# Expert weights in halves for the last two units, and two weight loads moved ahead of the token gathers

## The reference

```python
t = h2.reshape(T, D)                       # 512 x 1024
# group of 4, then top 2 of its 8 experts -> combine (T, 32), two entries per row
for e in range(N_EXPERTS):                 # 32
    hid = jax.nn.silu(t @ w_gate_exp[e]) * (t @ w_up_exp[e])     # 1024 -> 256
    y = y + combine[:, e:e + 1] * (hid @ w_down_exp[e])          # 256 -> 1024
```

## Time and profile before

| | us |
|---|---|
| median of 3 runs | 719.07 |
| lowest and highest | 716.56 and 719.19 |
| the profiled execution | 716.74 |
| its span on the core | 714.8 |
| TensorE busy in it | 651.9 (91%) |
| mean DMA rate over the span | 240 GB/s |

### The profile page before, as it was taken

The page is one execution under the profiler, slowest core; times in us unless marked ns, Lnnn a source line. Parts: engine busy times, 40 slices in busy tenths (PEclk is TensorE's granted clock), DMA queues, the critical chain, the costliest instruction groups (busy, mean ns, idle before and its releaser), DMA issues.

```text
span 714.8 us, 7294 instructions
## 1 busy us (share of the span) xinstructions
PE 651.9 (91%) x2526; PEld 313.5 (44%) x2526; DVE 381.5 (53%) x751; ACT 179.5 (25%) x366; POOL 90.2 (13%) x112
## 2 busy tenths in 40 slices
PE   0599999999999999999979999889999899898993
PEld 0454644444344444455644555434344443333331
DVE  3955265998877674417872338842323252232258
ACT  1430111133233434441121222112221121121132
POOL 1012312210011111000000000113111112111012
PEclk9999999999999999999999999999999999998997
DMA  9990826060602415070194028699999999999962
GB/s 324 393 378 6 273 81 235 0 235 0 206 31 83 153 25 212 1 244 29 37 387 195 29 77 335 247 417 419 415 423 419 420 418 418 420 419 420 412 262 117
DMA packets 50405, 171.85 MB, mean 240 GB/s; under 512 B 10176, under 2 KB 10176, under 8 KB 37440
## 3 DMA queue, kind: packets, MB, share of 16 engines
q1 hardware_dynamic: 42544, 159.24, 57.2%
q0 software_dynamic: 6016, 10.53, 3.9%
q10 hardware_dynamic: 1808, 1.61, 0.7%
HBM read 168.20 MB, written 13.64 MB: 254 GB/s over the span
## 4 chain that ended last, share of the span: by engine, by line
PE 75%; DMA 7%; DVE 7%; issue 6%; POOL 2%; ACT 1%; SPq 1%; DVEq 0%; ACTq 0%; POOLq 0%
PE psum L669 29%; PE psum L939 13%; PE psum L965 8%; PE psum L816 7%; DMA ring<-in_w_down_exp 4%; DVE work L1288 2%; PE psum L773 2%; PE psum L919 2%; DMA work<-h_rows,tok_t 2%; PE psum L793 2%; PE psum L781 1%; PE psum L738 1%; PE psum L731 1%; DMA posi<-in_positions 1%; PE psum L747 1%
## 5 line engine op out<-in xcount | busy, mean ns | idle before, releaser
L669 PE MATMUL psum<-ring,hT 128*128 128x512 f32 (+1 forms) x576 | 234.6, 561 | 0.0
L669 PEld LDWEIGHTS psum<-ring,hT 128*128 128x128 f32 x576 | 102.7, 191 | 119.2 <-issue 118.8
L939 PE MATMUL psum<-ring,hT 128*64 128x512 f32 (+1 forms) x352 | 84.9, 594 | 1.4 <-issue 1.4
L1700 DVE TENSOR_SCALAR work<-work 128x256 f32<-128x256 f32 x18 | 5.2, 291 | 121.0 <-PE psum L949 96.1
L939 PEld LDWEIGHTS psum<-ring,hT 128*64 128x64 f32 (+1 forms) x352 | 29.2, 142 | 54.6 <-issue 54.4
L1288 DVE SCALAR_TENSOR_TENSOR rows<-ring,sm,rows 128x512 f32<-128x512 f32 x64 | 51.3, 802 | 1.7
L965 PE MATMUL psum<-ring,work 128*64 128x512 f32 (+1 forms) x176 | 45.5, 620 | 3.3 <-DMA ring<-in_w_down_exp 2.6
L1184 ACT ACTIVATE work<-psum 128x256 f32<-128x256 f32 x18 | 6.9, 385 | 155.1 <-PE psum L939 155.1
L939 PE MATMUL psum<-rows,hT 128*64 128x512 f32 (+1 forms) x80 | 39.8, 656 | 6.6 <-issue 6.6
L1812 POOL TENSOR_TENSOR both_bufs<-both_bufs 128x256 f32<-128x256 f32 (+1 forms) x28 | 18.9, 673 | 180.4 <-DVE both_bufs L1349 156.7
L1349 DVE TENSOR_TENSOR both_bufs<-psum,cosT 128x512 f32<-128x512 f32 (+1 forms) x24 | 14.7, 614 | 48.9 <-PE psum L669 38.2
(11 more groups left out here) (270 smaller groups left out, 860.6 us busy)
## 6 DMA issues: line engine op xcount, KB each, us to landing
ring<-in_w_gate_exp SPq DMA_DIRECT2D x22, 1024.0 KB, 23.0
ring<-in_w_up_exp SPq DMA_DIRECT2D x22, 1024.0 KB, 26.0
ring<-in_w_down_exp SPq DMA_DIRECT2D x22, 1024.0 KB, 27.0
ring<-in_w_in SPq DMA_DIRECT2D x8, 2048.0 KB, 9.8
ring<-in_w_ada SPq DMA_DIRECT2D x8, 2048.0 KB, 14.8
ring<-in_w_ada SPq DMA_DIRECT2D x7, 1024.0 KB, 14.2
both_bufs<-in_w_gate_exp SPq DMA_DIRECT2D x5, 1024.0 KB, 27.0
both_bufs<-in_w_up_exp SPq DMA_DIRECT2D x5, 1024.0 KB, 28.8
```

The lines of the kernel that those rows point to most:

```text
L669: mm = pe.matmul(o[:, 0:width], hT3[:, k, b * P:(b + 1) * P], w[:, k, :], start=(k == 0), stop=(k == KD - 1))
L939: mm = pe.matmul(o[rows, :], XT[u % 2][:, k, rows], both(SLOT_OF[place])[:, k, :, :], start=(k == 0), stop=(k == KD - 1))
```

## The change

Two edits, both in what SyncE issues, with one new wait on TensorE.

The gate matrix of slot 4 is issued as soon as h2_ready and mod_done allow, and the down matrix of slot 1 behind `h2_out` and `res_sq`, both before the waits for the gathers; the up and down matrices of slot 4 stay behind them.

For units 16 and 17 gate and up of both places are loaded in halves of the contraction: first k = 0 to 3 of gate and up for both places, counted on `gu_in`, then k = 4 to 7, counted on the new `gu_rest`. `gate_up` of these units waits for `gu_rest` ahead of its product with k = 4.

```diff
+HALVED = NU - 2
...
+        gu_rest = [sem(f"gu_rest{i}") for i in range(NU - HALVED)]
...
+        def load_half(sp, e, s, part, signal):
 
-            w = KD * F
+            w = KD * F // 2
             at = gate_and_up(s)
-            sp.dma_start(at[:, 0:w], pick(wg_d, e)).then_inc(signal, 16)
-            sp.dma_start(at[:, w:2 * w], pick(wu_d, e)).then_inc(signal, 16)
+            for m, weights in enumerate((wg_d, wu_d)):
+                sp.dma_start(at[:, (2 * m + part) * w:(2 * m + part + 1) * w],
+                             pick(weights, e)[:, part * w:(part + 1) * w]).then_inc(signal, 16)
...
+            sp.wait_ge(h2_ready, NB)
+            sp.wait_ge(mod_done, 8)
+            load_gate(sp, RING, RING, gu_in[RING])
             sp.wait_ge(h2_out[1], 16 * (NB // 2))
             sp.wait_ge(res_sq, NB)
+            load_down(sp, 1, 1, down_in[1])
             for u in range(GATHERS):
                 sp.wait_ge(xg_in[u], 16)
-            load_down(sp, 1, 1, down_in[1])
-            sp.wait_ge(h2_ready, NB)
-            sp.wait_ge(mod_done, 8)
-            load_gate_up(sp, RING, RING, gu_in[RING])
+            load_up(sp, RING, RING, gu_in[RING])
             load_down(sp, RING, RING, down_in[RING])
...
+                    if UNIT_OF[place] < HALVED:
+                        sp.wait_ge(gu_mm, u + 1)
+                        load_gate_up(sp, named[place], SLOT_OF[place], gu_in[SLOT_OF[place]])
+                if LET_IN.get(u, []) and UNIT_OF[LET_IN[u][0]] >= HALVED:
                     sp.wait_ge(gu_mm, u + 1)
-                    load_gate_up(sp, named[place], SLOT_OF[place], gu_in[SLOT_OF[place]])
+                    for place in LET_IN[u]:
+                        load_half(sp, named[place], SLOT_OF[place], 0, gu_in[SLOT_OF[place]])
+                    for place in LET_IN[u]:
+                        load_half(sp, named[place], SLOT_OF[place], 1, gu_rest[UNIT_OF[place] - HALVED])
...
                 for k in range(KD):
+                    if u >= HALVED and k == KD // 2:
+                        pe.wait_ge(gu_rest[u - HALVED], 32 * len(UNITS[u]))
```

More of the change, by code:

```diff
@@ L481, in build, with load_gate, load_up @@
         SUM_BANK = (2, 4, 0, 6)
+        def load_gate(sp, e, s, signal):
+            sp.dma_start(gate_and_up(s)[:, 0:KD * F], pick(wg_d, e)).then_inc(signal, 16)
+        def load_up(sp, e, s, signal):
+            sp.dma_start(gate_and_up(s)[:, KD * F:2 * KD * F], pick(wu_d, e)).then_inc(signal, 16)
         def load_gate_up(sp, e, s, signal):
-            w = KD * F
+            load_gate(sp, e, s, signal)
+            load_up(sp, e, s, signal)
+        def load_half(sp, e, s, part, signal):
+            w = KD * F // 2
             at = gate_and_up(s)
-            sp.dma_start(at[:, 0:w], pick(wg_d, e)).then_inc(signal, 16)
-            sp.dma_start(at[:, w:2 * w], pick(wu_d, e)).then_inc(signal, 16)
+            for m, weights in enumerate((wg_d, wu_d)):
+                sp.dma_start(at[:, (2 * m + part) * w:(2 * m + part + 1) * w],
+                             pick(weights, e)[:, part * w:(part + 1) * w]).then_inc(signal, 16)
         def load_down(sp, e, s, signal):
```

## The result

The changed kernel takes 713.4 us in the median of 20 runs (710.86 to 716.78), the kernel before 717.26 us beside it (714.96 to 720.8, 20 runs). The ratio is 0.9947, 95% interval 0.9931 to 0.9963: 3.8 us faster. The profiled execution of the changed kernel took 715.57 us, with a span of 713.6.

The account below looks back on a forecast made before the run. The end was taken as set by the landing of the expert weights plus TensorE's work after it. Halves 2.6 us and early start 1.7 make 4.3 off the median 719.07: 714.8 us, range 711.8 to 718.6.

Parts of the forecast that it names:

- The early loads: Two 1 MB loads issued before the gathers: 5.0 us moved, of which the weight stream gains 1.7 us.
- the gather keeps its 3 us: First gather, clear of the two moved loads by 1.4 us, was still to take about 3.1 us.
- the hole: DMA queue dry from about 460 to 462.5 us, before the loads gate_up(0) frees; takes 3.3 of the 5.0 us.
- The halves: Units 16 and 17: 16 of 32 gate_up passes run before the second halves land; 2.6 us gained from this alone.
- The new tail: TensorE's end: gate_up(17) to end at 674.65 us, where it ended at 679.47, and down(17) at 684.7 against 688.99.
- The two pauses in gate_up(17): gate_up(17) was to wait 1.5 us for its first halves and 1.7 us for its second.
- The small rows: Half loads have 4 KB rows instead of 8 KB: 0.6 us cost in all, bounds 0 and 1.7.
- the 16 us: Upper cost of eight more DMAs by the Trainium skill's rule of about 2 us fixed cost each; prediction disagreed.
- The issues of SyncE: Eight added load issues, about 0.4 us each unloaded, were to cost nothing in front of a full queue.
- The last load: Last down load, read as landing at 680.4 us, was to land at 679.3, with down(17) starting at 681.05.
- The clock: Rival, chance 0.13: TensorE's clock falls in the tail after gate_up(17)'s two pauses; gain only 1.1 to 2.6 us.
- The collision with the gathers: Rival, chance 0.07: moved loads run into the gathers, gate_up(0) starts up to 5.6 us late; end 1.4 us later.

Follow-up runs that it names:

- e6: Changed kernel, but gate_up(16) and gate_up(17) wait for both halves before their first product; ratio 1.0005 against the kernel before.
- e10: The same kernel as e6, timed and profiled once more; ratio 0.9986 against the kernel before.
- e1: Changed kernel with only the halves, the first loads back behind the gathers; ratio 0.9967 against the kernel before.
- e5: Changed kernel with all four held-back loads ahead of the waits for the gathers; ratio 1.0002 against the kernel before.

## Why the prediction was right

The result, 3.8 us, lies 0.5 us from the forecast of 4.3, inside its own range, and the profile gives 4.0. The forecast time of 714.8 us is 1.4 too high for another reason: it was counted from 719.07, the median of three runs, where the median of twenty is 717.26. Step by step:

- **The early loads, 1.7 us.** Measured alone 1.8. Every part of that sum stood in the profile: the loads end before the gather, the gather keeps its 3 us, the hole opens, speed is back about 2.5 us after the issue at 464.50. That one early load does as well as two, and a third nothing, shows that the gain is the time to the freed loads and not the megabytes moved.
- **The halves, 2.6 us.** Measured alone 2.5. The new tail, moved by the 2.8 us by which this execution's gather came late, was to have gate_up(17) end at 674.65 + 2.8 = 677.45 and down(17) at 684.7 + 2.8 = 687.5; it has 677.70 and 687.83. The two pauses in gate_up(17) were to be 1.5 and 1.7 us and are 1.45 and 1.53.
- **The small rows, 0.6 us.** 0.5 to 0.7 by the profiles of the two kernels that wait at the start, 0.65 by the rate over most of the halves. The medians allow about twice that. Neither is near the 16 us that the prediction set against it.
- **The issues of SyncE cost nothing.** They took place in front of a full queue, as forecast; unit 16's last down load went out at 661.10, 11.8 us later than before (2.8 of it the later gather), and still landed 18.0 us after, in its turn: 1.0 us sooner than before when counted from the gather, where 1.1 was forecast.
- **The last load.** Here the working read a row wrongly. It took the last down load, issued at 654.10, to land after 26.3 us, at 680.4. Two loads of that form were issued, at 653.67 and 654.10, and the trace has a time to landing for one of them only. The first row is of the kernel before, and the other two are of the kernel with the early loads alone, in which the two were issued at 654.70 and 655.12:

```profile
L492 SPq DMA_DIRECT2D ring<-in_w_down_exp x2: 333/2406/4479, 653.7 to 654.1; - x2
DMA to landing us min/median/max: 26.3/26.3/26.3
```

```profile
L508 SPq DMA_DIRECT2D ring<-in_w_down_exp x2: 333/2402/4472, 654.7 to 655.1; - x2
DMA to landing us min/median/max: 26.3/27.4/28.4
```

So 26.3 us belong to the first load, which landed at 680.0, and 28.4 to the last, which landed at 682.5; the last event of its landing stands at 682.49 in the trace. Counted from the gather's issue it then landed at 234.0 us before and at 232.8 in the changed kernel (684.09 less 451.27): 1.2 us sooner, where 1.1 was forecast. The shift was right, and the place from which it was counted was 2.1 us too early. With 682.5 - 1.1 = 681.4 in the place of 679.3, down(17) starts at 681.4 instead of 681.05 and ends at 685.05, a gain of 3.9 instead of 4.3; the profile has 4.0. In the changed kernel down(17) waited for that load and started at 684.18, where 681.4 + 2.8 is 684.2:

```profile
662.34 21.75 DMA ring<-in_w_down_exp
684.18 3.65 PE psum L991 x16
```

The reads of pair_rows, issued at 677.70 instead of 682.42 and so before the last landing, did not slow it. In e6 and e10 they go out later, 1.7 us before that landing, and the last load still takes its 21.7 us and lands at 232.8 and 232.9 from the gather. The rows of e6:

```profile
L508 SPq DMA_DIRECT2D ring<-in_w_down_exp x2: 375/1638/2900, 659.9 to 660.4; - x2
DMA to landing us min/median/max: 19.7/20.7/21.7
...
680.39 2.04 SPq L673 DMA_DIRECT2D ring<-pair_rows  x4
```
- **The rivals.** The clock did not fall in the changed kernel's tail: two pauses of 1.5 us with 3.6 us of work between them left it at 1.00 in all seven profiles that have them. The collision with the gathers was a true danger at 1.4 us of distance, as the kernel with three shows, but not for two loads.

## What to carry to other kernels

When a stream of transfers is the bound, as here, moving loads ahead pays only the time until the next load whose buffer is still in use; look for that load first, since it tells how much is worth moving and what else would have to be freed. A product whose operand lands in halves ends half a product after the landing, which is worth having only for the last consumers of the stream. To compare two profiles of kernels that share a long prefix, measure from the last event up to which both run alike. Where a row speaks for two loads, find out which one it times before a sum is built on it.

## What the runs showed of the hardware

The executions of the two kernels come in steps about 2.1 us apart: the kernel before near 715.2, 717.2 and 719.2 us, the changed one near 711.4, 713.5 and 715.7. The steps of some others, e1 and e5 above all, are less clear. The profiles show one place where such a step arises, in the short products between the output projection and the table of tokens. Windows of the kernel before and then of the changed one; the third number from the end is TensorE's granted clock:

```profile
434.00:436.00 2.00, 2.00 (x4) 0.86 (x3) 1.76 (x12) 0.22 (x1) 0.53 (x1) 0.59 1.01 426
436.00:438.00 2.00, 2.00 (x4) 0.81 (x3) 1.69 (x10) 0.00 (x0) 0.00 (x0) 0.56 1.00 352
438.00:440.00 2.00, 2.00 (x6) 0.81 (x5) 1.86 (x14) 0.21 (x1) 0.00 (x0) 1.00 0.97 383
```

```profile
434.00:436.00 2.00, 2.00 (x11) 2.00 (x11) 0.68 (x1) 0.29 (x1) 0.53 (x1) 0.50 1.01 426
436.00:438.00 2.00, 2.00 (x4) 0.97 (x4) 1.69 (x11) 0.22 (x1) 0.00 (x0) 0.50 1.00 397
438.00:440.00 2.00, 2.00 (x3) 0.73 (x3) 1.69 (x10) 0.00 (x0) 0.00 (x0) 0.50 0.89 342
```

In the second the clock stays at 1.2 GHz (0.50) until after 440 us, in the first until before 438. From SyncE's first load of this stage (425.36 and 426.11) to the gather's issue it is 23.09 us in the one and 25.16 in the other. Of the twelve profiles of this study seven have 23.1 us there, four 25.2 and one 25.5: a step of 2.1 us in between. The low clock goes with it: from 426 to 442 us it adds up to 3.4 us or to none in the seven profiles with 23.1, and to about 10 us in the other five. It is not the change: of the ten kernels with early loads five have 23.1, and the step is there when the first moved load goes out, 13.6 us after the stage's first load in the five with the longer stretch and 10.2 to 11.5 in the other five. A second shift lies before this stage: its first load was issued between 423.67 and 426.50 us in the twelve profiles, and where that arises was not looked for. The gain moves all the steps alike, and nothing that was varied here sets the step on which an execution falls, so that the medians of 12 executions of one kernel, e6 and e10, could lie 1.1 us apart. The Trainium skill, "TensorE: Matmul & The Clock Gate", says in its Part 1 that the same kernel runs a different number of its products at the low clock from run to run. It says so of a kernel's start; here the low stretch lies in the middle, and the twelve profiles agree: they have none, 3.4 or about 10 us of it in a stretch of code that they share.
